# Masks of the inverses, state additions of the scan and the whole rotary embedding move to GpSimd in a four-layer forward pass

## What is computed

```python
def partial_rope(t, pos):          # the first 16 of each head's 64 features
    t1, t2 = tr[..., :half], tr[..., half:]
    rot = jnp.concatenate([t1 * cos - t2 * sin, t2 * cos + t1 * sin], axis=-1)
    return jnp.concatenate([rot, t[..., ROPE_DIM:]], axis=-1)

# nsa_mixer
s_cmp = jnp.einsum('bgrsd,bgcd->bgrsc', qh, k_cmp) * SCALE    # q without rotation
q_rot = partial_rope(qh, pos)
ks, kw = partial_rope(ks, pos), partial_rope(kw, pos)

def rwkv7_step(state, inp):
    sa = jnp.einsum('bhvk,bhk->bhv', state, -kk_t)
    state = (state * w_t[:, :, None, :] + sa[..., None] * (kk_t * a_t)[:, :, None, :]
             + v_t[..., None] * k_t[:, :, None, :])
    y = jnp.einsum('bhvk,bhk->bhv', state, r_t)
```

## Time and profile before

| | us |
|---|---|
| median of 3 runs | 1861.16 (1857.23 to 1862.93) |
| the profiled execution | 1861.29 |
| its span, first to last instruction | 1859.5 |
| TensorE busy | 1774.6 |
| VectorE busy | 956.5 |
| GpSimd busy | 701.0 |
| mean granted clock of TensorE | 0.978 |

### The profile page before, as it was taken

One profiled execution on the slowest core, in us unless ns is written; L12 is line 12 of the kernel. 1 busy time (PEld: TensorE's weight loads), 2 busy tenths in 40 slices (PEclk: granted clock), 3 DMA queues, 4 the chain that ended last, 5 costly groups with the idle time before them and its releaser, 6 DMA issues.

```text
span 1859.5 us, 28324 instructions
## 1 busy us (share of the span) xinstructions
PE 1774.6 (95%) x11768; PEld 1426.3 (77%) x11768; DVE 956.5 (51%) x1642; ACT 535.3 (29%) x1082; POOL 701.0 (38%) x333
## 2 busy tenths in 40 slices
PE   8999998999889989889999999999998999999999
PEld 5678777877766767767888888877786688888887
DVE  6676247666646355665656561133334366565411
ACT  3111113444323445543322220034223332222100
POOL 4343101000244132135655554452224475555542
PEclk9999999999899999999999999998999899999999
DMA  5222130000132321122332323221112123232332
GB/s 172 79 80 88 32 103 3 3 2 2 59 115 73 112 85 63 40 91 70 102 102 91 103 92 101 93 94 46 62 53 68 57 93 102 93 100 94 99 100 70
DMA packets 43505, 143.54 MB, mean 77 GB/s; under 512 B 5305, under 2 KB 7115, under 8 KB 43250
## 3 DMA queue, kind: packets, MB, share of 16 engines
q1 hardware_dynamic: 43378, 141.73, 23.3%
HBM read 139.07 MB, written 4.08 MB: 77 GB/s over the span
## 4 chain that ended last, share of the span: by engine, by line
PE 63%; DVE 5%; ACT 3%; issue 1%; POOL 1%; DVEq 0%; ACTq 0%; POOLq 0%
PE all_p_bank L206 19%; PE all_p_bank L207 18%; PE all_p_bank L208 18%; DVE l_sc L2478 1%; PE all_p_bank L2177 1%; PE all_p_bank L2390 1%; PE all_p_bank L2153 1%; DVE l_mx L2484 1%; PE all_p_bank L2419 0%; PE all_p_bank L2857 0%; PE all_p_bank L1904 0%; PE all_p_bank L2852 0%; DVE b_whi L180 0%; PE all_p_bank L2839 0%; POOL b_wlo L187 0%
## 5 line engine op out<-in xcount | busy, mean ns | idle before, releaser
L187 POOL TENSOR_TENSOR b_wlo<-b_raw,b_whi 128x1024 fp32r<-128x1024 f32 x238 | 580.6, 2443 | 782.7 <-DVE b_whi L180 778.8
L206 PE MATMUL all_p_bank<-b_hi,b_whi 128*128 128x512 f32 x1248 | 507.6, 407 | 11.4 <-issue 6.1
L207 PE MATMUL all_p_bank<-b_lo,b_whi 128*128 128x512 f32 x1248 | 489.6, 392 | 0.0
L208 PE MATMUL all_p_bank<-b_hi,b_wlo 128*128 128x512 f32 x1248 | 489.5, 392 | 0.0
L180 DVE CAST b_whi<-b_raw 128x1024 fp32r<-128x1024 f32 x238 | 186.2, 789 | 447.8 <-PE all_p_bank L208 430.3
L206 PEld LDWEIGHTS all_p_bank<-b_hi,b_whi 128*128 128x128 f32 x1248 | 236.5, 189 | 80.1 <-issue 25.4
L208 PEld LDWEIGHTS all_p_bank<-b_hi,b_wlo 128*128 128x128 f32 x1248 | 236.2, 189 | 51.0
L207 PEld LDWEIGHTS all_p_bank<-b_lo,b_whi 128*128 128x128 f32 x1248 | 236.5, 189 | 50.3 <-issue 5.1
L206 PE MATMUL all_p_bank<-f_mhi,b_whi 128*128 128x512 f32 x352 | 136.9, 389 | 0.0
L207 PE MATMUL all_p_bank<-f_mlo,b_whi 128*128 128x512 f32 x352 | 136.9, 389 | 0.0
L208 PE MATMUL all_p_bank<-f_mhi,b_wlo 128*128 128x512 f32 x352 | 136.9, 389 | 0.0
(11 more groups left out here) (452 smaller groups left out, 2667.1 us busy)
## 6 DMA issues: line engine op xcount, KB each, us to landing
b_raw<-in_w_up SPq DMA_DIRECT2D x88, 512.0 KB, 3.6
b_raw<-in_w_down SPq DMA_DIRECT2D x44, 512.0 KB, 3.7
b_raw<-in_w_in SPq DMA_DIRECT2D x32, 512.0 KB, 3.7
b_raw<-in_w_out SPq DMA_DIRECT2D x24, 512.0 KB, 3.7
b_raw<-in_w_gla SPq DMA_DIRECT2D x22, 512.0 KB, 3.6
b_raw<-in_w_diff SPq DMA_DIRECT2D x20, 512.0 KB, 3.7
b_raw<-in_w_mem SPq DMA_DIRECT2D x8, 512.0 KB, 3.8
all_x<-in_x SPq DMA_DIRECT2D x8, 256.0 KB, 5.4
```

The source lines that it names most:

```text
L187: self.nc.gpsimd.tensor_tensor(self.lo[:, n % SLOTS, :], self.raw[:, n % RAWS, :], self.hi[:, n % SLOTS, :].bitcast(F32), ALU.subtract).th ...
L206: nc.tensor.matmul(acc, lhsT=left[0], rhs=right[0], start=first, stop=False)
L207: nc.tensor.matmul(acc, lhsT=left[0], rhs=right[1], start=False, stop=False)
L208: return nc.tensor.matmul(acc, lhsT=left[1], rhs=right[0], start=False, stop=last)
```

## The change

The masks of the levels (L1634) are made by GpSimd. The two additions of the identity at level 0 become one: w = mb + I stays on VectorE, TensorE transposes w itself, and ScalarE's copy of that goes straight into z. The addition s1 = s + kv of the scan goes to GpSimd, for the first seven chunks (the last had no use). The rotation is done by GpSimd altogether: six tiles "turned" are filled with zeros, 24 transfers bring eight rows each of l1c_ct to the partners' partitions, the signs now lie in the table of sin, and a rope step is two products and an addition on GpSimd. The product with swap, its table and its transfer go. The scale of q, 1/8, goes into the evacuation of the projection. In the list of sparse steps, rope 0 and 1 stand behind the two inputs, and rope 3, 4 and 5 a place or so further forward or back.

```diff
-    order = [("rope", 0, 0), ("rope", 1, 0), ("gates", 0, 0), ("inputs", 0, 0), ("inputs", 1, 0)]
+    order = [("gates", 0, 0), ("inputs", 0, 0), ("inputs", 1, 0), ("rope", 0, 0), ("rope", 1, 0)]
...
-    order += [("values", 0, 0), ("scores", 0, 0), ("scores", 1, 0), ("rope", 2, 0), ("softmax", 0, 0),
-              ("rope", 3, 0), ("turn", 0, 0), ("rope", 4, 0), ("turn", 1, 0), ("rope", 5, 0), ("read", 0, 0), ("read", 1, 0)]
+    order += [("values", 0, 0), ("scores", 0, 0), ("scores", 1, 0), ("rope", 2, 0), ("rope", 3, 0), ("softmax", 0, 0),
+              ("rope", 4, 0), ("turn", 0, 0), ("rope", 5, 0), ("turn", 1, 0), ("read", 0, 0), ("read", 1, 0)]
...
         sp.dma_start(m.w2[:, 1, :, :], k["w2v"]).then_inc(self.i_w2, 16)
+        sp.wait_ge(self.s_blank, 6)
+        for n, tile in enumerate(self.jobs):
+            for r0 in (0, HD):
+                for a, b in ((r0, r0 + 8), (r0 + 8, r0)):
+                    sp.dma_start(m.turned[n][a:a + 8, :], m.ct[b:b + 8, tile, :]).then_inc(self.i_turned[n], 16)
         sp.dma_start(m.mask_add[:, :, :], k["cmp_maskadd"]).then_inc(self.i_ma, 16)
...
                 pool.wait_ge(*self.projected)
+                for turned in m.turned:
+                    nc.gpsimd.memset(turned[:, :], 0.0).then_inc(self.s_blank, 1)
...
             if what == "gates":
+                pe.wait_ge(*self.projected)
                 pe.wait_ge(self.s_gs, 1)
-                pe.wait_ge(self.s_t2, 2)
...
+    def rope(self, pool, n):
+        nc, m, x = self.nc, self.m, self.m.ct[:, self.jobs[n], :]
...
+        pool.wait_ge(self.i_turned[n], 64)
         if n >= 2:
+            pool.wait_ge(self.s_rot, n - 1)
+        nc.gpsimd.tensor_tensor(m.t1[:, n % 2, :], x, m.cos[:, :], ALU.mult).then_inc(self.s_t1, 1)
+        nc.gpsimd.tensor_tensor(m.t2[:, n % 2, :], m.turned[n][:, :], m.sin[:, :], ALU.mult).then_inc(self.s_t2, 1)
+        pool.wait_ge(self.s_t1, n + 1)
+        pool.wait_ge(self.s_t2, n + 1)
         if n == 2:
+            pool.wait_ge(self.s_cs, 1)
+        nc.gpsimd.tensor_tensor(x, m.t1[:, n % 2, :], m.t2[:, n % 2, :], ALU.add).then_inc(self.s_rot, 1)
...
         if kv == 0:
             dve.wait_ge(self.i_pos, 16)
-            dve.wait_ge(self.s_rot, 2)
+            dve.wait_ge(*self.projected)
...
         for what, n, i in self.order:
+            if what == "level":
+                if n == 0:
+                    pool.wait_ge(self.i_sm, 16)
+                    pool.wait_ge(self.i_la, 16)
+                    pool.wait_ge(self.s_pc, 16)
+                    self.masked(pool, 0)
+                if n + 1 < 4 * self.levels:
+                    self.masked(pool, n + 1)
+            if what == "as" and n < NCH - 1:
+                pool.wait_ge(self.s_st, n + 1)
+                if n:
+                    pool.wait_ge(self.s_tmp, n)
+                self.nc.gpsimd.tensor_tensor(m.s1[:, :, :], m.s[:, n % 2, :, :], m.kv[:, :, n, :], ALU.add
+                                             ).then_inc(self.s_s1, 1)
...
         m, lv, i = self.m, n // 4, n % 4
-        pe.wait_ge(self.s_mb, n + 1)
+        if lv:
+            pe.wait_ge(self.s_mb, n + 1)
+        else:
+            pe.wait_ge(self.s_wv, n + 1)
...
+                left = m.mb[rows, n % 2, c, :] if lv else m.w[rows, i, c, :]
                 rhs = m.z[rows, i, c, :] if lv else self.k["ident"][rows, rows]
...
-                nc.scalar.activation(m.g[:, n % 2, :, :], b[n % 2][:, :].rearrange("p (c t) -> p c t", t=CH), ACT.Copy
+                out = m.g[:, n % 2, :, :] if n >= 4 else m.z[:, n, :, :]
+                nc.scalar.activation(out, b[n % 2][:, :].rearrange("p (c t) -> p c t", t=CH), ACT.Copy
...
-    def masked(self, dve, n):
+    def masked(self, pool, n):
         m, lv, i = self.m, n // 4, n % 4
-        if n >= 2:
-            dve.wait_ge(self.s_lg, n - 1)
+        if n >= 6:
+            pool.wait_ge(self.s_lg, n - 1)
         if 2 <= n < 6:
-            dve.wait_ge(self.s_wv, n - 1)
...
+            pool.wait_ge(self.s_wv, n - 1)
+        self.nc.gpsimd.tensor_tensor(m.mb[:, n % 2, :, :], m.abk[:, 0, i, :, :], self.mask(lv), ALU.mult).then_inc(self.s_mb, 1)
...
             nc.vector.tensor_tensor(m.w[:, i, :, :], m.mb[:, n % 2, :, :], eye, ALU.add).then_inc(self.s_wv, 1)
-            dve.wait_ge(self.s_gc, n + 1)
-            nc.vector.tensor_tensor(m.z[:, i, :, :], m.g[:, n % 2, :, :], eye, ALU.add).then_inc(self.s_z, 1)
```

More of the change, by code:

```diff
@@ L737, in __init__ @@
         self.w2, self.hid = s.sb("w2", [P, 2, 2, P]), s.sb("hid", [P, 2, 2, 2 * CMP_N])
-        self.swap, self.vc = s.sb("swap", [P, P]), s.sb("vc", [P, 2, HD])
+        self.vc = s.sb("vc", [P, 2, HD])
+        self.turned = [Shelf(nc, f"l1t{i}", where).sb("turned", [P, T])
+                       for i, where in enumerate((a + 4096, a + 6144, *range(a + 20480, a + 28672, 2048)))]
         self.xp = at("x", a + 36864, "xp", [P, 2, 2, CMP_N, CMP_B // 2])
@@ L2536 @@
     fresh: bool
+    scale: float = 1.0
 class Projection:
@@ L2562, in take, with features @@
         return [self.banks[i] for i in b], waits
-    def features(self, n, src, base, width, outs, row):
+    def features(self, n, src, base, width, outs, row, scale=1.0):
         self.nd += len(outs)
@@ L2616, in evacuate @@
             guard(dve, job.n + b)
-            self.nc.vector.tensor_tensor(out, job.banks[b][:, 0:job.width], row, ALU.mult).then_inc(self.s_evd, 1)
+            acc = job.banks[b][:, 0:job.width]
+            if job.scale == 1.0:
+                self.nc.vector.tensor_tensor(out, acc, row, ALU.mult).then_inc(self.s_evd, 1)
+            else:
+                self.nc.vector.scalar_tensor_tensor(out=out, in0=acc, scalar=job.scale, in1=row, op0=ALU.mult, op1=ALU.mult
+                                                    ).then_inc(self.s_evd, 1)
             yield
@@ L3509, in first_layer, with features @@
     n = ring.add(a["w_in1"])
-    def features(tiles):
+    def features(tiles, scale=1.0):
         nonlocal n
         for t in tiles:
-            proj.features(n, norm, 0, T, [t], row)
+            proj.features(n, norm, 0, T, [t], row, scale)
             n += 1
```

89 lines of the change are left out of this document (26 added, 63 removed).

## The result

The changed kernel took 1875.01 us (median of four runs, 1873.72 to 1875.07), the kernel before 1859.81 on the same chip: a ratio of 1.0079, 95% interval 1.0064 to 1.0094, slower. The profiled execution took 1875.07, its span 1873.3 against 1859.5, +13.8 us. The forecast was +8.7. (The title above says four layers; it is the one hybrid layer and two further ones.)

A forecast was written before the change was run, and what follows sets the result against it. TensorE was busy 95%, but VectorE was taken to bound some 30 us of layer one. 4.4 + 1.0 - 1.1 + 4.4 + 1.0 - 1.0 = +8.7 us on 1861.3 gave 1870.0 us; range 1861 to 1877 (own 1865.5 to 1874.5).

The forecast's parts named there:

- rival 2: Front: SyncE's queue bounds at 0.64 us an issue, TensorE stays longer on low clock; +13.9, 1875.2 us; chance 0.15.
- The new order: Front: position additions ahead of pair 1's evacuation start the hidden product at 241.7 instead of 237.28; +4.4 us.
- SyncE's queue: Front: 24 small transfers at 0.55 us ahead of w1v's loads delay w1v; +1.0 us, between 0 and 3.2.
- Scores to T: VectorE's first scores operation to the last pair's evacuation end (T): shorter without rotation 2; -1.1 us, -2.9 to 0.
- T to the second round: From T to the end (E) of the second round's product of tile 1: GpSimd's longer chain; +4.4 us.
- Clock: Thin stages: TensorE waits longer, so more slow clock may reach the dense part; +1.0 us, between 0 and +4.
- Scan: Scan: seven additions of 0.41 us leave VectorE, shortening TensorE's waits; -1.0 us, between -2.4 and 0.
- Signs: Expected in the new profile: first level product some 9 us behind the last pair, second round ending near 308.
- Rival 1: Scores to second round: VectorE's operations fit into GpSimd's pauses without exclusion; +2.3, 1863.6 us; chance 0.22.
- rival 3: VectorE's 30 us: GpSimd multiplies quicker than it adds; turns at 1.24 us, 0.7 gives 1855.4 us; chance 0.08.

The follow-up runs named there:

- e2_order: The changed kernel with the rotations of the two key tiles ahead of the positions' additions again; ratio to the kernel before 1.0062.
- e9_short: The change with 8 transfers, the positions' additions at their old place, and GpSimd's rotations 4 and 5 cut to 8 columns; 1858.88 us, one execution.
- e11_early: The change with 8 transfers, the positions' additions at their old place, and the query tiles' eight rotation products ahead of the scores; ratio to before 0.9972.
- e12_plain: e11_early with the identity part of the change undone as well; ratio to the kernel before 0.9973.
- e13_unident: The change with 8 transfers, the positions' additions at their old place, and the identity part undone; ratio to the kernel before 1.0025.

## Why the prediction was right and where it was wrong

The sign and the range held: 1875.0 in 1861 to 1877, slower. It lies half a microsecond above the forecast's own range, and on the number of rival 2; of a rise of 13.8 us in the spans the sum had 8.7, so the range held by 2 us. Term by term, in the profiled execution:

- **The new order, +4.4: measured +5.2** (242.5 against 237.3). The additions started at 233.65 as worked out (233.7); the 0.8 us more is pair 3 at the lower clock.
- **SyncE's queue, +1.0: this is the term with the largest error.** A copy was taken at 0.55 us and took 0.69 from issue to issue, above my upper bound of 0.64. The step between back-to-back copies of the same tensor was the nearer row; I went below it for no reason that a row gave. The 24 copies so take 3.3 us more than booked, and by as much the second hidden block comes later than forecast: 257.48 in place of 254.1, front +8.8 in place of +5.4. The wait for w1v shows only 1.6 us, because the first hidden products lost 1.9 to the clock meanwhile; at the full clock, by these rows, TensorE would have waited 3.5 and resumed at the same time. That the queue lies behind the order, with most of it hidden by it, was right: e2_order shows the 8.7 us that come out when the order is taken away.
- **Scores to T, -1.1: measured +0.4** (11.5 against 11.1), 1.5 too little. The collision was as foreseen: 1.65 and 1.47 us for the subtractions of the maximum, 1.70 for GpSimd's product. The pair products were booked at 1.1 us and took 1.84 (3.68 for two) at the lower clock.
- **T to the second round, +4.4: measured +5.0, with two errors that cancel in part.** The chain on GpSimd up to mask 4 was booked at 18.5 us and took 16.7; it runs without a gap and sets the end, as said, and e9_short and e11_early show it by taking the rotations out (16.3 and less for all of E - T). Its eleven operations lost 2.6 us to VectorE (16.5 against eleven of 1.26), where I had booked all of VectorE's 4.1 (3.8 by the row, which has 0.27 for both small ones together). One piece of it shows: the softmax's product with the mask, which I expected at 1.7 us or more, kept its 1.13; for the rest why less was lost I can only argue. In turn TensorE's last three steps, booked at 4.4, took 6.9 at the lower clock.
- **Clock, +1.0: the step that failed in kind.** It was booked as one small sum that reaches into the dense part. It came in the products behind each wait instead, in the stages that have their own terms: some 1.5 us in the last two pairs and 2.5 in the read and the product behind it, about 4 in all. (The 0.9 in pair 3 and 1.9 in the first hidden products cost nothing in the end, since w1v came no sooner.) Rival 2 (a queue at 0.64 us or more, TensorE waiting in the hidden products, longer on the lower clock, +4) had both mechanisms. That its +13.9 meets the measured +13.8 is luck in part: it had the front 1.2 and the scan 1.0 too low and the chain on GpSimd 1.8 too high. I gave it 0.15; the row of the copies spoke for more.
- **Scan, -1.0: measured 0**, from its first to its last step. Half-size additions lay beside the attention's work on TensorE; the waits of the earlier trace rows fell from 3.5 us to 2.6, and as the scan got no shorter, the rest came back elsewhere.
- **The sum.** Front +8.8, scores to T +0.4, T to the second round +5.0: +14.2 there, and 13.8 at the scan and in the span. Against 8.7 the front had 3.4 too little, scores to T 1.5, the second round 0.6 and the scan 1.0, while the clock's own 1.0 was too much, as was 0.4 between E and the scan.
- **Signs.** The first level product, expected some 9 us behind T, came at 5.5, behind the first addition of the identity. The second round ended at 313.8, not near 308. The stretch behind did not shrink.

The Trainium skill (SBUF — State Buffer, § Who interferes with whom) was weighed as the rule that speaks against the change, and the trace agrees with it on both sides: additions of two SBUF tiles take 1.72 us beside GpSimd's masks, while the evacuations with one PSUM input (L1510) stay at 0.69 and the reduction L1082 at 1.17, the same as before.

Rival 1 (no exclusion) is refuted by these rows, rival 3 by GpSimd's product: 1.27 us alone, above the 1.24 at which the sum was to turn. But its idea, that VectorE's relief there is worth something, is right once nothing stands between the masks: 15.0 us in e12_plain against 18.5 before.

What stays open: how much of the gain of e12_plain is the masks' and how much the rotations' (the masks alone, in the old order, cost; the rotations alone were tried only with the wait for the last pair left in); where the 3 us of e11_early's and e12_plain's gain lie that the stages don't show; and why e13_unident and e12_plain, both without the identity part, take 51.4 and 51.6 us for the scan.

## What to carry to other kernels

Work that moves to an idle engine is free only where it stands in that engine's order: ask what is queued behind it, not how busy the engine is. Here two rotations cost 4.6 us between the masks (E - T of 20.9 against 16.3) and nothing where GpSimd had been idle. Count the issues of a queue, not the bytes, and look whose load stands behind them. Whoever books a wait on TensorE should book the slower products behind it as well, unless they wait for something else anyway. Whoever takes work off an engine should take its waits along.
